# Recurrent stage of a hybrid layer: HBM loads in smaller pieces, each released by its own product

## What is computed

```python
    def step(state, inp):
        r_t, w_t, k_t, v_t, kk_t, a_t = inp
        sa = jnp.einsum('bhvk,bhk->bhv', state, -kk_t)
        state = (state * w_t[:, :, None, :]
                 + sa[..., None] * (kk_t * a_t)[:, :, None, :]
                 + v_t[..., None] * k_t[:, :, None, :])
        return state, jnp.einsum('bhvk,bhk->bhv', state, r_t)
    ...
    _, y = lax.scan(step, s0, tuple(map(seq_first, (r, decay, k, v, kk, a))))
    ...
    mean = jnp.mean(y, axis=-1, keepdims=True)
    var = jnp.mean(jnp.square(y - mean), axis=-1, keepdims=True)
    yn = ((y - mean) * lax.rsqrt(var + RWKV_GN_EPS)).reshape(bsz, length, RWKV_WIDTH)
    yn = yn * ln_w.astype(f32) + ln_b.astype(f32)
    bonus = (jnp.sum(r * k * r_k.astype(f32), axis=-1, keepdims=True) * v).reshape(bsz, length, RWKV_WIDTH)
    return ((yn + bonus) * g.astype(f32)).astype(p.dtype)
```

## Time and profile before

| what | value |
|---|---|
| median of 3 runs | 2808.72 us (2807.12 to 2809.67) |
| the profiled execution | 2791.34 us, its span 2789.6 us |
| PE busy over the span | 2570.4 us, 92% |
| DVE, ACT, POOL busy | 1561.6, 1314.9, 316.3 us |
| mean granted TensorE clock | 0.973 of full speed |
| bytes moved by DMA | 440.46 MB, mean 158 GB/s |

### The profile page before, as it was taken

How to read it: one execution, slowest core, us unless ns; L and a number is a source line. 1 busy time by engine, 2 the same in 40 slices (tenths; PEclk the granted TensorE clock), 3 DMA queues, 4 the chain that set the end, 5 groups by cost and what they waited for, 6 DMA issues and landing times. The chain is left out here.

```text
span 2789.6 us, 65043 instructions
## 1 busy us (share of the span) xinstructions
PE 2570.4 (92%) x27593; PEld 2142.2 (77%) x27593; DVE 1561.6 (56%) x2370; ACT 1314.9 (47%) x2266; POOL 316.3 (11%) x367
## 2 busy tenths in 40 slices
PE   6999999999989999989999999899895999999992
PEld 6989896777766766678889889778784788888882
DVE  4566664443035555544444444553325888888884
ACT  4655542222134444334444444562223777777771
POOL 0111222332000000001212122100000000000002
PEclk9999999999999999999999999999996999999996
DMA  4444342222122323222222101244345999999976
GB/s 110 152 166 139 128 149 74 92 92 74 40 94 71 95 64 137 79 62 62 59 56 60 56 21 33 63 128 136 116 181 210 389 394 398 395 394 397 394 302 257
DMA packets 160693, 440.46 MB, mean 158 GB/s; under 512 B 14343, under 2 KB 94873, under 8 KB 148145
## 3 DMA queue, kind: packets, MB, share of 16 engines
q1 hardware_dynamic: 144461, 381.94, 38.3%
q10 hardware_dynamic: 9060, 29.56, 2.8%
q0 software_dynamic: 6912, 25.17, 2.4%
HBM read 344.22 MB, written 92.41 MB: 157 GB/s over the span
## 5 line engine op out<-in xcount | busy, mean ns | idle before, releaser
L2599 DVE TENSOR_TENSOR ex_wL<-wx,ex_wH 128x2048 fp32r<-128x2048 f32 x192 | 436.1, 2286 | 46.5 <-ACT ex_wH L2503 42.4
L2503 ACT CAST ex_wH<-wx 128x2048 fp32r<-128x2048 f32 x192 | 366.3, 1911 | 94.2 <-PE ex_bank L2399 70.8
L2397 PE MATMUL ex_bank<-ex_wH,ex_xTH 128*128 128x512 f32 x512 | 200.4, 391 | 2.4 <-DVE ex_xTL L2604 2.4
L2399 PE MATMUL ex_bank<-ex_wL,ex_xTH 128*128 128x512 f32 x512 | 200.0, 391 | 0.0
L2398 PE MATMUL ex_bank<-ex_wH,ex_xTL 128*128 128x512 f32 x512 | 200.0, 391 | 0.0
L709 PE MATMUL ph_acc<-ph_wH,uH 128*104 128x512 f32 x480 | 192.7, 401 | 6.5 <-DVE ph_wL L721 6.5
L709 PE MATMUL ph_acc<-ph_wH,uL 128*104 128x512 f32 x480 | 189.7, 395 | 0.0
L709 PE MATMUL ph_acc<-ph_wL,uH 128*104 128x512 f32 x480 | 189.6, 395 | 0.0
L413 PE MATMUL pf_acc<-uH,pf_wH 128*128 128x348 f32 x648 | 160.7, 356 | 6.4 <-DVE pf_wL L533 6.4
L413 PE MATMUL pf_acc<-uL,pf_wH 128*128 128x348 f32 x648 | 139.0, 323 | 0.0
L413 PE MATMUL pf_acc<-uH,pf_wL 128*128 128x348 f32 x648 | 138.6, 322 | 0.0
(11 more groups left out here) (397 smaller groups left out, 6779.2 us busy)
## 6 DMA issues: line engine op xcount, KB each, us to landing
wx<-in_expert_w_gate SPq DMA_DIRECT2D x32, 2048.0 KB
wx<-in_expert_w_up SPq DMA_DIRECT2D x32, 2048.0 KB
wx<-in_expert_w_down SPq DMA_DIRECT2D x32, 2048.0 KB
s_y<-ex_y ACTq DMA_DIRECT2D x32, 512.0 KB, 10.1
fw<-in_w_in SPq DMA_DIRECT2D x27, 512.0 KB
hw<-in_w_in SPq DMA_DIRECT2D x6, 2048.0 KB, 10.2
s_qkT<-ph_stg ACTq DMA_DIRECT2D x4, 2080.0 KB, 6.9
mb_gt<-s_pT SPq DMA_DIRECT2D x16, 512.0 KB, 3.5
```

Source lines behind the costliest of these rows:

```text
L2397: nc.tensor.matmul(out, aH, bH, start=first, stop=False)
L2399: return nc.tensor.matmul(out, aH, bL, start=False, stop=last)
L2503: nc.scalar.copy(wH[:, w, part], raw(j, s)[:, part]).then_inc(w_high, 1)
L2599: nc.vector.tensor_tensor(wL[:, w, part], raw(j, s)[:, part], wH[:, w, part], ALU.subtract).then_inc(w_low, 1)
```

## The change

The loads of a pair are cut from 10 transfers of 128 partitions into 40 of 32 partitions (133 KB), and the loads of the group norm's inputs from 4 into 8 (143 or 117 KB, one head's half of one tensor each). Each piece waits for a product of its own: pieces go out behind products 1, 2, 3 and 5 of successive chunks, four per chunk. The counts of the semaphores that the readers wait for rise with the number of pieces (640 for 160, 128 for 64). The chunk at which each group of loads begins is now a number in the call.

```diff
         def _(sp):
-            def load(d, n):
+            STEP = (1, 2, 3, 5)
+
+            def after(ch, s):
+                sp.wait_ge(seq_pe, seq_done(ch + s // len(STEP), STEP[s % len(STEP)]))
+
+            def load(d, ch):
                 z = d % 2
-                e, k = divmod(n, 5)
-                dst, j = ((BK[z][:, e, 0], BHAT), (KR[z][:, e, 0], KAP), (KR[z][:, e, 1], RHAT), (BK[z][:, e, 1], KHAT), (V[z][:, e], VAL))[k]
-                if d > 1 or n > 0:
-                    sp.wait_ge(seq_pe, seq_done(NCH * (d - 1) - 1 + n, 5))
-                sp.dma_start(dst, c.rwD[2 * d + e, j]).then_inc(x_in[z], 16)
-
-            def load_rest(gi):
+                s = 0
+                for e in range(2):
+                    for dst, j in ((BK[z][:, e, 0], BHAT), (KR[z][:, e, 0], KAP), (KR[z][:, e, 1], RHAT), (BK[z][:, e, 1], KHAT), (V[z][:, e], VAL)):
+                        for rows in (slice(32 * n, 32 * n + 32) for n in range(4)):
+                            after(ch, s)
+                            sp.dma_start(dst[rows], c.rwD[2 * d + e, j, rows]).then_inc(x_in[z], 16)
+                            s += 1
+
+            def load_rest(gi, ch):
                 d, x = divmod(gi, 2)
                 if gi >= 2:
                     sp.wait_ge(*gn_at(gi - 2, "gate"))
                 lo_, hi = GRP[x][0] * TC, GRP[x][1] * TC
+                s = 0
                 for dst, j in ((bon[x], BONUS), (g[x], GATED)):
-                    for e in range(2):
-                        sp.dma_start(dst[half(e), :, 0:hi - lo_],
-                                     c.rwD[2 * d + e, j, :, lo_:hi].rearrange("(h p) t -> p h t", h=2)).then_inc(e_in[x], 16)
-
-            load_rest(0)
-            for gi in range(1, 2 * ND):
-                if gi % 2 == 1 and gi // 2 + 1 < ND:
-                    for n in range(10):
-                        load(gi // 2 + 1, n)
-                load_rest(gi)
+                    for e, h in PAIRS:
+                        after(ch, s)
+                        sp.dma_start(dst[half(e), h, 0:hi - lo_], c.rwD[2 * d + e, j, half(h), lo_:hi]).then_inc(e_in[x], 16)
+                        s += 1
+
+            load_rest(0, 0)
+            load(1, 2)
+            load_rest(1, 12)
+            for d in range(2, ND + 1):
+                load_rest(2 * d - 2, NCH * (d - 1) - 3)
+                if d < ND:
+                    load(d, NCH * (d - 1))
+                load_rest(2 * d - 1, NCH * (d - 1) + 10)
```

More of the change, by code:

```diff
@@ L1349, in _ @@
             sp.wait_ge(early_in, 128 + OPEN)
-            sp.wait_ge(e_in[1], 64 * ND + OPEN)
+            sp.wait_ge(e_in[1], 128 * ND + OPEN)
         @block.tensor
@@ L1359, in masked @@
                     if ch % NCH == 0:
-                        pe.wait_ge(x_in[z], 160 * ((d + 1) // 2) + OPEN)
+                        pe.wait_ge(x_in[z], 640 * ((d + 1) // 2) + OPEN)
                     if ch > 0:
@@ L1609, in norm @@
                     pool.wait_ge(*gn_at(gi, "e2"))
-                    pool.wait_ge(e_in[x], 64 * d + 64 + OPEN)
+                    pool.wait_ge(e_in[x], 128 * d + 128 + OPEN)
                     ins = nc.gpsimd.tensor_tensor(yw[:, :, 0:hi - lo_], yw[:, :, 0:hi - lo_], bon[x][:, :, 0:hi - lo_], ALU.add)
```

## The result

| | median | executions |
|---|---|---|
| before | 2809.19 us | 2807.12 to 2812.7 (4) |
| changed | 2789.69 us | 2786.39 to 2792.2 (4) |

The ratio is 0.9935, 95% interval 0.9916 to 0.9953: 18 us or 0.65% faster, between 13 and 24. The two kernels were compared twice more, each time on one chip: 0.9941 (0.9922 to 0.9959) and 0.994 (0.9925 to 0.9954). So the gain is some 17 us.

The account below looks back on a forecast made before the run. TensorE bounds the recurrence, pausing when instruction fetches queue behind loads. Of 20.5 us of load cost, pieces keep 7.5 and the weights' burst 2, so 11 us off 2808.7 gives 2797.7 us, range 2791 to 2810.

Parts of the forecast that it names:

- What bounds the stage, and that pauses pass one to one: Recurrence: TensorE bounds it, busy 516.56 of 558 us; its 45.2 us of instruction pauses pass into the time almost fully.
- A fetch that finds data ahead comes late: Recurrence: a 16 KB instruction fetch queued behind load data is delayed; pauses 0.20 us each when quiet, up to 1.68.
- The group norm's loads and the clock: Recurrence: 8 fetches in the group norm's loads cost 11.8 us over quiet ones, a clock fall 1.5 more.
- The pair loads: Recurrence: whole 520 KB loads cost 5.2 us for fetches just behind one and 2.0 for others beside one.
- The pieces' cost: Recurrence after the change: 77 fetches, 45% behind a piece, still lose 7.5 us, between 4 and 15.
- From the trace to the time: Whole kernel: the traced 2791.3 us lay 17 under the median, so only the 11 us difference came off 2808.7.
- The clock's term: Recurrence: after the 2.38 us pause the granted clock fell to 0.69, costing one chunk 1.5 us.
- The weights' burst kept 2 us: End of recurrence: the next stage's eight weight transfers, moved to chunk 72, still delay one or two fetches, 1.5 to 3.
- Deadlines and late gates: Recurrence: loads keep 31 us of cover, costing nothing; three late group norm gates put three pieces in a row, counted in 7.5.
- What the profile would show: Recurrence: pauses sum near 34 us, those over 1 us nearly gone, packet intervals at most 4.5 us, loading-chunk pauses 0.2 to 0.5.
- no gain: Recurrence: pieces delay fetches as much in total as whole loads; 2806 to 2809 us; chance 0.24.
- slower: Recurrence: each of 77 fetches meets a piece and pays 0.43, 33 us; 15 us slower, 2824; chance 0.12.

Follow-up runs that it names:

- e9: Against the changed kernel: pair loads whole again (10 of 520 KB), each issued when an instruction packet is just beginning; 0.9932 of the kernel before.
- e10: Same transfers as e9, but each pair load issued when the next instruction packet is 1.6 to 2.3 us off; 1.0004 of the kernel before.
- e6: Against the changed kernel: the four pieces of one tensor go out in a row behind one product; 0.9947 of the kernel before.
- e7: Against the changed kernel: pair loads in 20 halves of 64 partitions (266 KB), behind products 1 and 3; 0.9958 of the kernel before.
- e4: Against the kernel before: only the group norm's inputs in 8 pieces, pair loads still 10 transfers of 520 KB; ratio 0.9975.
- e3: Against the kernel before: only the pair loads in 40 pieces of 133 KB, group norm's inputs as before; ratio 0.9971.
- e8: Against the changed kernel: the next stage's eight weight transfers also go out each behind its own product; 0.9933 of the kernel before.
- e5: The changed kernel without the loads for pairs 2 and 3 and group norms 2 to 7; 0.9921 of the kernel before, stage 532.1 us.
- e13: Against the kernel before: nothing split, but each load issued singly, behind a product where an instruction packet is just beginning; ratio 0.993.
- e1: The kernel before, unchanged, timed against itself and traced again; ratio 1.001, traced execution 2802.4 us.
- e2: The changed kernel, unchanged, timed and traced again on one chip with the kernel before; ratio 0.9941, traced execution 2785.8 us.
- e14: The kernel before, unchanged, traced a fourth time; ratio 1.0002, traced execution 2804.5 us.

## Why the prediction was right or wrong

*What bounds the stage, and that pauses pass one to one*: right. In the changed kernel a chunk less its pauses still takes 6.0 to 6.3 us with the same places at 7.0 to 7.6; and a stage less its pauses is 494.4 to 497.3 us in the 13 traces with one fall of the clock or none, and 498.8 to 500.9 in the four with two to four.

*A fetch that finds data ahead comes late*: right, shown by e9 against e10 with size and bytes held. How the amount that is ahead enters is not shown: e6 missed, and e7 can't be told from either side.

*The group norm's loads and the clock*: 13.3 us less their share of the pieces (2.6) and the weights (2) was 8.7; e4 measured 7.0. Right in size, with some luck: the terms were read from the one trace in which the part of the stage with these loads was 4 to 8 us shorter than in the other three.

*The pair loads*: this is the step that failed. The prediction had "12 x 0.43 = 5.2, 33 x 0.06 = 2.0", 7.2 us in all, less two thirds of the 7.5 for the pieces (4.9), so a net 2.3. e3 measured 8.1 us (4.5 to 12). How the error divides between the two terms is known only in part.

The pieces' cost was too high by most readings. By time the changed kernel at 0.994 lies 0.1% above e9, some 2 us, though the intervals overlap. By the traces, where 18 of the 30 pair loads go out, the pieces take 0.4 us more than no loads at all; the forecast's share would be 2.9. The cost before is less clear. By the same 18 loads it is 3.5 us, for a share of 4.3 in the forecast. By time whole loads at the old moments (e4, 0.9975) cost 0.43% more than at good ones (e9, 0.9932), 12 us with an interval of some 6 to 18, on two chips and with some of the norm's pieces moved as well. Beside the pair loads the first trace wasn't light, so that isn't the reason. Why the time gives 8.1 us for e3 where these chunks give less stays open.

*From the trace to the time*: the prediction saw that the traced execution lay 17 us under the median and took "the difference alone". That assumed that the 17 us lay elsewhere. Execution less stage shows that such differences lie in the very stage that was being summed: in four traces of the kernel before, the stage goes from 539.9 to 548.7 us (mean 545.0), in three of the changed one from 530.1 to 534.6 (mean 532.1). The means differ by 12.9 us, the first two traces by 5.3. Of the 12.9, 4.1 are beside the pair loads (the first two columns above) and 8.8 in the rest; of the 5.3 they are 3.0 and 2.3. The clock's term, 1.5 us by one chunk, is 1 to 4 falls in the four traces, and what a stage takes less its pauses is 500.9, 499.9 and 499.6 us in the other three for 495.6.

*The weights' burst kept 2 us*: e8 shows no more than can be measured. *Deadlines and late gates*: no wait for a load appears on TensorE, as forecast. *What the profile would show*: the sum of pauses near 34 us came in two of three traces (35.0, 34.4), 39.2 in the first; the pauses over 1 us went from 12 or 13 to 3, 1 and 3. Not as forecast: in the first trace of the changed kernel 15 intervals between instruction packets are over 4.5 us, the longest 5.87 (22 in the first trace before, the longest 5.87 as well), and 34 of its 81 pauses are over 0.5 us.

*The rivals*: the measured gain of 13 to 24 us excludes both "no gain" and "slower". Both rested on a cost of 0.43 us for a fetch that meets a piece, for 15 or 33 us in all, where the runs leave the pieces 0 to some 7. As for the rule in the Trainium skill, "Runtime: NRT & Kernel Launch", Instruction fetch mechanics, that a 16 KiB boundary is mostly hidden: beside loads this stage doesn't bear it out, as pauses of up to 3.23 us and the gain itself show, and without any load a fetch still costs 0.23 us in e5. The Trainium skill, "DMA: Bandwidth & Descriptors", Rules for kernel authors, advises large transfers for bandwidth. Bandwidth doesn't bound this stage (16.6% of the engines), and e13, with its transfers whole, has the gain too.

Open: why executions of the kernel before spread over 17 us on one chip (2791.1 to 2808.2 in e1) and those of the changed one over 8 (2777.7 to 2785.8 in e2), beyond that large pauses leave room for chance; why the timed ratio gives 17 us where the traces' means give 13; whether it is the size of the pieces, the time between them or the chance of where they fall that helps, as e6, e7 and e9 don't agree on one; and whether the changed kernel's pieces cost 0 (stage of e5) or up to 7 us (stages of e9 and e13, time of e5), as one trace of each can't tell this.

## What to carry to other kernels

Where TensorE runs many small instructions, count its instruction packets in the DMA queues and look at where its "issue" pauses end: a load that fills the queues when a packet is due is paid by TensorE, however early the load itself is wanted. Issue large loads singly and behind an instruction at which a packet has just begun; here this gave as much as smaller pieces behind successive products. Small ones in a row (four of 133 KB in e6, eight of 128 KB in the changed kernel) cost nothing that the times could tell, though e6's trace has more pauses. And before a term is summed from one trace, ask whether the traced execution is typical: if it lies far from the median, look for the difference in the stage at hand first; here all 17 traces had it there.

## What the runs showed of the hardware

- The moment at which 30 loads of 520 KB start moved a 2.8 ms program by 0.7% (0.9932 and 1.0004), with bytes, sizes and order equal.
- A pause of 3.23 us was followed by a granted clock of 0.50 for 3 us. In the 17 traces, 12 pauses of 1.82 to 3.23 us were followed by such a fall (chunks of 9.0 to 12.0 us), and others of up to 2.50 us (e14) were not.
- In chunks without any load, instruction fetches still cost TensorE 0.23 us each (86 fetches in e5).
- Splitting by 32 partitions or by 260 columns made no difference that could be measured (0.994 and 0.9937).
